# First gate unit of the two gated MLPs computed by token halves, in 128-column products

## The chip, the cores and the metric

The kernel runs on one core of one Trainium2 chip. The metric is device microseconds of one execution. The kernel before takes 1236.24 us, the median of 3 runs (1235.91 to 1247.31).

## The reference

Two transformer blocks act on 256 tokens of width 1024, batch 1, in float32. The second block is the one that the change touches:

```python
def swiglu(h, w_gate, w_up, w_down):
    return (jax.nn.silu(h @ w_gate) * (h @ w_up)) @ w_down
...
        h = modulate(rmsnorm(x, norm_ffn1[l]), sh1, sc1)
        x = x + 0.5 * g1[:, None, :] * swiglu(h, ffn1_w_gate[l], ffn1_w_up[l], ffn1_w_down[l])
        h = modulate(rmsnorm(x, norm_mix[l]), sh2, sc2)
        x = x + g2[:, None, :] * hybrid_mixer(h, ...)
        h = modulate(rmsnorm(x, norm_ffn2[l]), sh3, sc3)
        x = x + 0.5 * g3[:, None, :] * swiglu(h, ffn2_w_gate[l], ffn2_w_up[l], ffn2_w_down[l])
    return rmsnorm(x, norm_final)
```

`rmsnorm` divides each token's row by its root mean square and multiplies by a weight; `modulate` is `h * (1 + scale) + shift` with one scale and one shift per channel. The gated MLPs (ffn1, ffn2) have an inner width of 2816.

## The kernel before

**Data.** The 256 tokens are two halves t = 0, 1 of 128, which lie on the 128 partitions of `x` and `xn` (tokens by channels). A stage's input is transposed into `ah` and `al` (channels by tokens, 8 tiles of 128 channels): `ah` is the value rounded to fp32r, `al` the rest. Weights are cut into units of 128 x 2048 and split in the same way into `whi` and `wlo`: ScalarE (ACT) writes `whi` (L593), VectorE (DVE) then writes `wlo` (L1039). Each matrix product is three products, `whi*ah`, `whi*al` and `wlo*ah`, with a weight load of its own each. Three units are held at a time, units are split in program order, and the second unit of ffn1 is split on both engines only after the whole input of ffn1 is ready (`splits(U_FFN1 + 1)`).

**A unit of the gate or the up matrix** is `a_unit` (L1782 to L1784): two blocks of 128 output channels, each 8 channel tiles of 3 products with 256 columns (all tokens), so 48 products. The products go into one PSUM bank. The pairs of channel tiles wait for `in_ready`, one by one, in the first block.

**The entry of a gated MLP.** The part before ends with four quarters of the residual, (t, v) = (0,0), (0,1), (1,0), (1,1) with v a half of the channels. DVE adds each to `x` (ffn1: `gained_parts`, L1299, with the product by the final norm's weight, L1302; ffn2: `gated_part`, L1351, L1352). ACT squares each with a running sum (`part_squares`; in ffn1 two squares a quarter, L657 and L661, in ffn2 one). After the second quarter of a token half comes the root chain: small DVE operations (`part_rstd`, L1275 to L1285) with a square root on ACT (L668) in their midst. Then the token half is scaled: t = 0 by ACT (L703), t = 1 half by ACT and half by DVE (L1289). TensorE (PE) makes the gate's rows (L2050), then runs `part_T`: it transposes token half 0 three times over, 24 transposes (L1900) whose results are overwritten, and then both token halves, 16 transposes (L1881), into banks 4 to 7. After each pair of channel tiles ACT multiplies by the modulation's gain and adds the shift, 2 operations of 256 columns into `tmp2`, which holds two pairs (L638), and DVE casts to `ah` and subtracts for `al` (L1101, L1102), 512 columns each. PE's first product waits for the first pair.

**The mixer's entry** has another form already: the first pair of channel tiles of token half 0 goes ahead. `half_gained` (ACT, L678, 2 operations of 128 columns) stands between the two squares of token half 1, `half_split` (DVE, L1110, L1111, 256 columns each) after the last residual addition and ahead of the root chain, and PE starts products with it (L2208) before token half 1 is transposed (L2217).

Each engine takes its instructions strictly in the order in which they are written; semaphores join them.

Of the kernel before, what the change touches and what calls it, by code (L numbers as in the profile page):

```python
# [7 lines left out]
ALU = mybir.AluOpType  # L8
# [7 lines left out]
P = 128  # L16
# [73 lines left out]
Y_BANK = [[5, 6], [4, 7]]  # L90
PART = {"ffn1": 0, "mix": 1, "ffn2": 2, "out": 3}
# [17 lines left out]
def build(nc, t_in, out):  # L109
    g = t_in  # L110
    with ExitStack() as ctx:
# [472 lines left out]
        def _(act):  # L584
# [37 lines left out]
            def gained(stage_name, dst, gain, shift=None, npairs=4, bank_of=TBANK, ntiles=CT, first=0):  # L622

                for j in range(first, npairs):
# [4 lines left out]
                    for q in range(n):  # L629
                        c = 2 * j + q  # L630
                        n0 = P if stage_name == "mix" and j == 0 else 0
# [42 lines left out]
            def half_gained(gain, shift):  # L674

                act.wait_ge(half_tr, 1)
                for c in range(2):
                    ins = A.activation(tmp2[:, 0, c * S:c * S + P], ps[:, TBANK[0], c * S:c * S + P], ACT.Identity,  # L678
                                       scale=gain(c), bias=shift(c))
                ins.then_inc(half_hi, 1)  # L680

            def part_square(b, t, v):

                cols = slice(512 * v, 512 * v + 512)
                act.wait_ge(x_part, 4 * b + 2 * t + v + 1)
                return A.activation(xn[:, t, cols], x[:, t, cols], ACT.Square, scale=D ** -0.5,
                                    accum_out=sums[:, 2 * t + v:2 * t + v + 1])

            def part_norm(b, ahead=None):

                root_table()
                for t in range(TT):
                    if ahead and t == 1:
                        splits(U_TAIL + 1)
                        part_square(b, t, 0)
                        half_gained(*ahead)
                        part_square(b, t, 1).then_inc(sq_part, 1)
                    else:
                        part_squares(b, t)
                    root(b, t)  # L700
                    act.wait_ge(r_part, 2 * b + t + 1)
# [90 lines left out]
            def chunk(cs, used_units, b, silu, buf):  # L792
# [6 lines left out]
                if silu:  # L799
                    A.activation(hr, bank(b), ACT.Silu).then_inc(gated, 1)  # L800
# [98 lines left out]
            part_norm(PART["ffn1"])  # L899
            act.wait_ge(mod_done, 3)  # L900
            mod = lambda k: (lambda c: mgain[:, k, c:c + 1], lambda c: modT[:, k, c:c + 1])
            gained("ffn1", ah, *mod(0))
# [102 lines left out]
            part_norm(PART["ffn2"])  # L1005
# [16 lines left out]
        def _(dve):  # L1022
# [65 lines left out]
            def gained(stage_name, hi, lo, gain, shift=None, npairs=4, bank_of=TBANK, ntiles=CT, first=0):  # L1088

                for j in range(first, npairs):  # L1090
                    dve.wait_ge(in_hi, PAIR0[stage_name] + j + 1)
                    if stage_name == "mix" and j == 0:
                        ins = half_split(1)
# [12 lines left out]
            def half_split(t):  # L1106

                tt = slice(t * P, t * P + P)
                v = tmp2[:, 0].rearrange("p (c n) -> p c n", c=2)[:, :, tt]
                link(V.tensor_copy(ah[:, 0:2, tt], v))  # L1110
                return V.tensor_tensor(al[:, 0:2, tt], v, ah[:, 0:2, tt].bitcast(F32), ALU.subtract)  # L1111
# [180 lines left out]
            def gained_parts(idx, k):  # L1292

                dve.wait_ge(nb_landed, 16)
                for t in range(TT):
                    for v in range(2):
# [57 lines left out]
            def gated_parts(idx, b):  # L1354

                for t in range(TT):
                    gated_part(idx, b, t)
                    if t == 1 and b == PART["mix"]:
                        dve.wait_ge(half_hi, 1)
                        half_split(0).then_inc(half_in, 1)  # L1360
                    part_rstd(b, t)
                part_scale(b)

# [392 lines left out]
        def _(pe):  # L1756
# [350 lines left out]
            def swiglu(n0, c0, stage_name, gates):  # L2107
# [23 lines left out]
                pair(n0, None, c0, 4, stage_name)  # L2131
# [65 lines left out]
            part_T(PART["ffn1"])  # L2197
# [14 lines left out]
            def mix_T(t, cs, ready=None):  # L2212
                for c in cs:
                    if ready and c in ready:
                        pe.wait_ge(*ready[c])
# [185 lines left out]
```

## Time and profile before

| | us |
|---|---|
| median of 3 runs | 1236.24 |
| lowest, highest | 1235.91, 1247.31 |
| profiled execution | 1238.66 |
| its span, first to last instruction | 1237.0 |
| PE busy | 1201.1 |
| DVE busy | 828.4 |
| ACT busy | 597.9 |
| mean granted clock of PE | 0.993 |

The profile is of one execution. A product's length in it is the time from its start until its result has landed; products are pipelined, so what one costs in a run of products is the distance between two starts. PE is TensorE's products, PEld its weight loads. "Idle before, <- engine tile line" says how long the engine stood still and what ended the wait.

### The profile page before, as it was taken

Reading aid. Unit: us, or ns where it says so; the run is one execution under the profiler, and the core shown is the slowest. Engines: PE = TensorE matmul, PEld = TensorE weight load, DVE = VectorE, ACT = ScalarE, POOL = GpSimd, SP = SyncE. Lnnn points to the kernel's source line nnn. Section 1 sums busy time; section 2 is a strip of 40 time slices with the busy share of each in tenths; the row PEclk is TensorE's granted clock in tenths of the full one; section 3 lists DMA queues with packets and bytes.
Section 4 is the critical chain, followed back from the end, with each engine's and each line's share of the span. In section 5 each row is a group of like instructions: output and inputs, shape, how many; then the busy total and the mean of one; then the engine's idle time right before and its main releaser. Section 6 shows DMA issues by size and latency. Waiting matters only on the chain.

```text
span 1237.0 us, 19961 instructions
## 1 busy us (share of the span) xinstructions
PE 1201.1 (97%) x7963; PEld 1091.9 (88%) x7963; DVE 828.4 (67%) x1113; ACT 597.9 (48%) x789; POOL 70.4 (6%) x106
## 2 busy tenths in 40 slices
PE   8999999999999999999999999999998999999997
PEld 7897899999888889999979999998987888999996
DVE  6676777777766769777665654547985866554445
ACT  5545543444545554444365344446746745443433
POOL 9100011110000001111000000000000000000000
PEclk9999999999999999999999999999998999999999
DMA  7633699888363259888544555544561043565560
GB/s 247 220 132 109 211 334 306 302 288 280 113 205 125 81 204 337 287 290 301 178 137 170 188 188 183 176 155 161 187 205 69 1 170 115 195 201 172 175 213 35
DMA packets 143240, 236.38 MB, mean 191 GB/s; under 512 B 6357, under 2 KB 106950, under 8 KB 143174
## 3 DMA queue, kind: packets, MB, share of 16 engines
q1 hardware_dynamic: 130402, 196.73, 47.7%
q0 software_dynamic: 10400, 37.77, 8.6%
q10 hardware_dynamic: 2372, 0.96, 0.3%
q8 instruction: 46, 0.75, 0.3%
q14 instruction: 20, 0.16, 0.0%
HBM read 234.37 MB, written 1.05 MB: 190 GB/s over the span
## 4 chain that ended last, share of the span: by engine, by line
PE 90%; DVE 5%; ACT 3%; issue 1%; DMA 0%; DVEq 0%; ACTq 0%
PE ps L1782 13%; PE ps L1784 13%; PE ps L1783 13%; PE ps L1857 10%; PE ps L1859 10%; PE ps L1861 10%; PE ps L1794 2%; PE ps L1796 2%; PE ps L1795 2%; PE ps L1946 1%; PE ps L2043 1%; PE ps L1948 1%; PE ps L1947 1%; PE ps L2028 1%; PE ps L1821 1%
## 5 line engine op out<-in xcount | busy, mean ns | idle before, releaser
L1039 DVE TENSOR_TENSOR wlo<-raw,whi 128x2048 fp32r<-128x2048 f32 (+2 forms) x187 | 421.4, 2259 | 187.2 <-ACT whi L593 186.7
L593 ACT ACTIVATE whi<-raw 128x2048 fp32r<-128x2048 f32 (+2 forms) x187 | 352.6, 1888 | 246.5 <-PE ps L1861 146.5
L1782 PE MATMUL ps<-ah,whi 128*128 128x256 f32 x1392 | 396.1, 285 | 9.9 <-DVE al L1102 3.8
L1783 PE MATMUL ps<-al,whi 128*128 128x256 f32 x1392 | 394.5, 283 | 0.0
L1784 PE MATMUL ps<-ah,wlo 128*128 128x256 f32 x1392 | 394.5, 283 | 0.0
L1782 PEld LDWEIGHTS ps<-ah,whi 128*128 128x128 f32 x1392 | 267.6, 192 | 14.5 <-issue 6.9
L1783 PEld LDWEIGHTS ps<-al,whi 128*128 128x128 f32 x1392 | 267.6, 192 | 1.8
L1784 PEld LDWEIGHTS ps<-ah,wlo 128*128 128x128 f32 x1392 | 267.6, 192 | 0.0
L1857 PE MATMUL ps<-whi,hh 128*128 128x512 f32 x376 | 117.2, 393 | 0.0
L1859 PE MATMUL ps<-wlo,hh 128*128 128x512 f32 x376 | 116.3, 390 | 0.0
L1861 PE MATMUL ps<-whi,hl 128*128 128x512 f32 x376 | 115.9, 389 | 0.0
L1859 PEld LDWEIGHTS ps<-wlo,hh 128*128 128x128 f32 x376 | 70.6, 188 | 15.2
L1861 PEld LDWEIGHTS ps<-whi,hl 128*128 128x128 f32 x376 | 70.6, 188 | 15.2
L1428 DVE SCALAR_TENSOR_TENSOR stage<-stage,cact 128x1024 f32<-128x1024 f32 x63 | 80.7, 1281 | 1.4
L1857 PEld LDWEIGHTS ps<-whi,hh 128*128 128x128 f32 x376 | 67.5, 189 | 11.2
L804 ACT ACTIVATE work<-ps 128x512 f32<-128x512 f32 x32 | 19.2, 598 | 115.3 <-PE ps L1784 115.3
L566 POOL DMA_DIRECT2D stage<-in_w_ada_dram x72 | 38.3, 532 | 445.2 <-PE ps L1981 154.6
L800 ACT ACTIVATE work<-ps 128x512 f32<-128x512 f32 x22 | 13.2, 599 | 87.9 <-PE ps L1784 87.9
L1375 DVE TENSOR_TENSOR hl<-work,hh 128x512 fp32r<-128x512 f32 x54 | 37.4, 692 | 18.1 <-ACT hh L802 16.9
L1370 DVE TENSOR_TENSOR work<-work,ps 128x512 f32<-128x512 f32 x22 | 15.1, 687 | 50.9 <-ACT work L800 50.9
L716 ACT ACTIVATE work<-ps,nmx 128x128 f32<-128x128 f32 x40 | 14.7, 368 | 63.8 <-DVE nmx L1138 63.8
L1857 PE MATMUL ps<-whi,ah 128*128 128x512 f32 x120 | 37.3, 381 | 0.0
(392 smaller groups left out, 1666.3 us busy)
## 6 DMA issues: line engine op xcount, KB each, us to landing
stage<-in_w_ada_dram POOLq DMA_DIRECT2D x72, 512.0 KB, 6.6
raw<-in_w_up_dram SPq DMA_DIRECT2D x32, 1024.0 KB, 6.9
raw<-in_w_down_dram SPq DMA_DIRECT2D x32, 1024.0 KB, 7.6
raw<-in_ffn_w_gate_dram SPq DMA_DIRECT2D x22, 1024.0 KB, 5.1
raw<-in_ffn_w_up_dram SPq DMA_DIRECT2D x22, 1024.0 KB, 5.1
raw<-in_ffn_w_down_dram SPq DMA_DIRECT2D x22, 1024.0 KB, 5.0
raw<-in_moba_w_qkv_dram SPq DMA_DIRECT2D x11, 1024.0 KB, 7.0
raw<-in_w_in_dram SPq DMA_DIRECT2D x10, 1024.0 KB, 5.0
```

The source lines that it names most:

```text
L566: pool.dma_start(aslot[:, c % ADA_RING], ada[:, c, bass.ds(b * D, D)]).then_inc(a_landed[c % ADA_RING], 16)
L593: A.activation(whi[:, s, 0:size], raw[:, s, 0:size], ACT.Copy).then_inc(w_hi, 1)
L1039: V.tensor_tensor(wlo[:, s, 0:size], raw[:, s, 0:size], whi[:, s, 0:size].bitcast(F32), ALU.subtract).then_inc(w_lo, 1)
L1375: V.tensor_tensor(flat(hl[:, buf]), hs, flat(hh[:, buf]).bitcast(F32), ALU.subtract).then_inc(h_ready, 1)
L1428: V.scalar_tensor_tensor(aacc, v, cact[:, c:c + 1], aacc, ALU.mult, ALU.add).then_inc(a_sum, 1)
L1782: T.matmul(o, wmh, xh[:, c], start=(c == 0), stop=False)
L1783: T.matmul(o, wmh, xl[:, c], start=False, stop=False)
L1784: ins = T.matmul(o, wml, xh[:, c], start=False, stop=(c == CT - 1))
L1794: T.matmul(o, wmh, xh[:, c], start=(c == 0), stop=False)
L1857: T.matmul(o, xh[:, c, tt], wh[:, k, v:e], start=(first and k == 0), stop=False)
L1859: T.matmul(o, xh[:, c, tt], wl[:, k, v:e], start=False, stop=False)
L1861: ins = T.matmul(o, xl[:, c, tt], wh[:, k, v:e], start=False, stop=(last and k == kn - 1))
```

## The change

In ffn1 and ffn2 the first unit of the gate matrix is computed in four blocks of 128 output channels by 128 tokens (`ffn_entry`): block(channels 0, tokens 0), then the transposes of token half 1, then block(1, 0), block(0, 1), block(1, 1), each 24 products of 128 columns. Its result goes into bank 2 in place of bank 4. The 24 extra transposes go; token half 0 is transposed once. Token half 0 of all four pairs is scaled, shifted and split ahead: on ACT `half_gained` for pairs 0 and 1 between the squares of (1,0) and (1,1), pair 2 behind the squares of (1,1), pair 3 behind the root; on DVE pairs 0, 1 and 2 behind the last residual addition and ahead of the root chain, pair 3 behind the scaling. The scaling and splitting of token half 1 keeps its place and its number of operations, in 128 and 256 columns in place of 256 and 512. The mixer's entry does the same work as before.

```diff
+HALF_BASE = {0: 0, 1: 4, 2: 5}
+HALVES = {"ffn1": 4, "mix": 1, "ffn2": 4}
...
-            def half_gained(gain, shift):
-
-                act.wait_ge(half_tr, 1)
-                for c in range(2):
-                    ins = A.activation(tmp2[:, 0, c * S:c * S + P], ps[:, TBANK[0], c * S:c * S + P], ACT.Identity,
+            def half_gained(b, j, gain, shift):
+
+                act.wait_ge(half_tr, HALF_BASE[b] + j + 1)
+                if j >= 2:
+                    act.wait_ge(half_in, HALF_BASE[b] + j - 1)
+                for q in range(2):
+                    c = 2 * j + q
+                    ins = A.activation(tmp2[:, j % 2, q * S:q * S + P], ps[:, TBANK[j], q * S:q * S + P], ACT.Identity,
                                        scale=gain(c), bias=shift(c))
                 ins.then_inc(half_hi, 1)
...
-                    if ahead and t == 1:
-                        splits(U_TAIL + 1)
+                    if t == 1:
+                        if b == PART["mix"]:
+                            splits(U_TAIL + 1)
                         part_square(b, t, 0)
-                        half_gained(*ahead)
+                        half_gained(b, 0, *ahead)
+                        if b != PART["mix"]:
+                            half_gained(b, 1, *ahead)
                         part_square(b, t, 1).then_inc(sq_part, 1)
+                        if b != PART["mix"]:
+                            half_gained(b, 2, *ahead)
                     else:
                         part_squares(b, t)
                     root(b, t)
+                    if t == 1 and b != PART["mix"]:
+                        half_gained(b, 3, *ahead)
...
+            def half_ahead(b, j):
+
+                dve.wait_ge(half_hi, HALF_BASE[b] + j + 1)
+                half_split(j, 0).then_inc(half_in, 1)
...
+                    if t == 1:
+                        for j in range(3):
+                            half_ahead(0, j)
                     part_rstd(0, t)
                 part_scale(0)
+                half_ahead(0, 3)
...
-            def part_T(b):
+            def half_T(t, cs, ready=None):
+                for c in cs:
+                    if ready and c in ready:
+                        pe.wait_ge(*ready[c])
+                    o = ps[:, TBANK[c // 2], (c % 2) * S + t * P:(c % 2) * S + (t + 1) * P]
+                    ins = T.transpose(o, xn[:, t, c * P:(c + 1) * P], ident[:])
+                    if c % 2 == 1:
+                        ins.then_inc(tr_done if t else half_tr, 1)
+
+            def ffn_entry(b, n, stage_name):
+
+                wh, wl = w_view(whi, slot(n), CT, AW), w_view(wlo, slot(n), CT, AW)
+
+                def block(m, t):
+                    tt = slice(t * P, (t + 1) * P)
+                    o = ps[:, 2, m * S + t * P:m * S + (t + 1) * P]
+                    for c in range(CT):
+                        if m == 0 and c % 2 == 0:
+                            pe.wait_ge(in_ready if t else half_in, (PAIR0[stage_name] if t else HALF_BASE[b]) + c // 2 + 1)
+                        wmh, wml = wh[:, c, m * P:(m + 1) * P], wl[:, c, m * P:(m + 1) * P]
+                        T.matmul(o, wmh, ah[:, c, tt], start=(c == 0), stop=False)
+                        T.matmul(o, wmh, al[:, c, tt], start=False, stop=False)
+                        ins = T.matmul(o, wml, ah[:, c, tt], start=False, stop=(c == CT - 1))
+                    return ins
 
                 pe.wait_ge(xn_act, 2 * b + 1)
-                for _ in range(3):
-                    for c in range(CT):
-                        T.transpose(ps[:, TBANK[c // 2], (c % 2) * S:(c % 2) * S + P], xn[:, 0, c * P:(c + 1) * P],
-                                    ident[:])
-                transposes(xn, [(xn_act, 2 * b + 1), {0: (xn_dve, b + 1), 4: (xn_act, 2 * b + 2)}])
+                half_T(0, range(CT))
+                unit_wait(n)
+                pe.wait_ge(x_part, 4 * b + 3)
+                block(0, 0)
+                half_T(1, range(CT), {0: (xn_dve, b + 1), 4: (xn_act, 2 * b + 2)})
+                block(1, 0)
+                block(0, 1)
+                block(1, 1).then_inc(w_used, 1)
...
-                pair(n0, None, c0, 4, stage_name)
+                ffn_entry(PART[stage_name], n0, stage_name)
+                a_unit(n0 + 1, slot(n0 + 1), 5, ah, al)
```

The order of the instructions shows it on two engines. On ACT, at the entry of ffn1, from the scaling of token half 0 to the split of the second weight unit (`stage,sums` is the square's scratch and its sum, `newt` the small values of the root chain, `work` is `tmp2`), before:

```order
L703 ACTIVATE xn<-xn,newt 128x1024
L657 ACTIVATE stage,sums<-x 128x512
L661 ACTIVATE stage,sums<-xn 128x512
L657 ACTIVATE stage,sums<-x 128x512
L661 ACTIVATE stage,sums<-xn 128x512
L668 ACTIVATE newt<-newt 128x1
L703 ACTIVATE xn<-xn,newt 128x512
L638 ACTIVATE work<-ps,modT,mgain 128x256 x8
L593 ACTIVATE whi<-raw 128x2048
```

and now:

```order
L720 ACTIVATE xn<-xn,newt 128x1024
L691 ACTIVATE stage,sums<-x 128x512
L695 ACTIVATE stage,sums<-xn 128x512
L683 ACTIVATE work<-ps,modT,mgain 128x128 x4
L691 ACTIVATE stage,sums<-x 128x512
L695 ACTIVATE stage,sums<-xn 128x512
L683 ACTIVATE work<-ps,modT,mgain 128x128 x2
L670 ACTIVATE newt<-newt 128x1
L683 ACTIVATE work<-ps,modT,mgain 128x128 x2
L720 ACTIVATE xn<-xn,newt 128x512
L640 ACTIVATE work<-ps,modT,mgain 128x128 x8
L595 ACTIVATE whi<-raw 128x2048
```

Four of the new operations stand ahead of the last squares, two between them and the root.

On DVE, at the same place, from the last residual quarter to the scaling of token half 1, before:

```order
L1299 SCALAR_TENSOR_TENSOR x<-ps,rsq,x 128x512
L1302 TENSOR_TENSOR xn<-x,nB 128x512
L1275 TENSOR_SCALAR newt<-sums 128x1
L1276 TENSOR_SCALAR newt<-sums 128x1
L1277 TENSOR_SCALAR newt<-newt 128x1
```

and now:

```order
L1321 SCALAR_TENSOR_TENSOR x<-ps,rsq,x 128x512
L1324 TENSOR_TENSOR xn<-x,nB 128x512
L1127 CAST ah<-work 128x2x128
L1128 TENSOR_TENSOR al<-work,ah 128x2x128
L1127 CAST ah<-work 128x2x128
L1128 TENSOR_TENSOR al<-work,ah 128x2x128
L1127 CAST ah<-work 128x2x128
L1128 TENSOR_TENSOR al<-work,ah 128x2x128
L1297 TENSOR_SCALAR newt<-sums 128x1
L1298 TENSOR_SCALAR newt<-sums 128x1
L1299 TENSOR_SCALAR newt<-newt 128x1
```

The six operations of three half pairs stand between the residual and the root chain of token half 1.

## Rows read from the trace of the kernel before

**Rows 1.** The page, part 4: shares of the span in the chain that ended last

```profile
PE 90%; DVE 5%; ACT 3%; issue 1%; DMA 0%; DVEq 0%; ACTq 0%
```

**Rows 2.** Timeline, PE, first entry: start, length, engine, line, op, tiles, [idle before]

```profile
640.97 1.88 PE L2050 MATMUL ps<-stage,cum 128*128 128x512 f32 x4
...
642.68 2.78 PE L1900 MATMUL ps<-ident,xn 128*128 128x128 f32 x24
...
646.99 1.09 PE L1881 MATMUL ps<-ident,xn 128*128 128x128 f32 x8 [0.65 <-DVE xn L1289]
...
649.88 0.36 PE L1782 MATMUL ps<-ah,whi 128*128 128x256 f32 x1 [1.80 <-DVE al L1102]
...
657.48 0.28 PE L1782 MATMUL ps<-ah,whi 128*128 128x256 f32 x1
...
657.60 0.28 PE L1783 MATMUL ps<-al,whi 128*128 128x256 f32 x1
```

**Rows 3.** Timeline, PE, entry of the second gated MLP

```profile
1036.07 1.91 PE L1881 MATMUL ps<-ident,xn 128*128 128x128 f32 x16
...
1039.72 0.36 PE L1782 MATMUL ps<-ah,whi 128*128 128x256 f32 x1 [1.74 <-DVE al L1102]
...
1046.69 0.28 PE L1782 MATMUL ps<-ah,whi 128*128 128x256 f32 x1
```

**Rows 4.** Timeline, PE: pairs of 512 and 176 columns, then pairs of 512

```profile
851.26 0.51 PE L1859 MATMUL ps<-wlo,ah 128*128 128x512 f32 x2
...
851.60 0.51 PE L1861 MATMUL ps<-whi,al 128*128 128x512 f32 x2
...
990.50 0.61 PE L1857 MATMUL ps<-whi,bh 128*128 128x512 f32 x2
...
990.95 0.62 PE L1859 MATMUL ps<-wlo,bh 128*128 128x512 f32 x2
```

**Rows 5.** Timeline, weight loads: two products of 64 columns a row

```profile
970.73 0.30 PEld L2357 LDWEIGHTS ps<-stage,work 128*128 128x128 f32 x2
...
970.95 0.30 PEld L2358 LDWEIGHTS ps<-stage,work 128*128 128x128 f32 x2
```

**Rows 6.** Timeline, all engines, mixer entry: its half pieces, then the first product

```profile
840.86 0.79 ACT L678 ACTIVATE work<-ps,modT,mgain 128x128 f32<-128x128 f32 x2
...
841.54 0.62 ACT L686 ACTIVATE xn<-x 128x512 f32<-128x512 f32 x1
...
841.68 0.29 DVE L1110 CAST ah<-work 128x256 fp32r<-128x256 f32 x1 [0.46 <-ACT work L678]
...
842.00 0.42 DVE L1111 TENSOR_TENSOR al<-work,ah 128x256 fp32r<-128x256 f32 x1
...
842.35 0.21 DVE L1279 TENSOR_SCALAR newt<-sums 128x1 f32<-128x1 f32 x1
...
842.58 0.55 PE L2208 MATMUL ps<-whi,ah 128*128 128x512 f32 x2 [1.28 <-DVE al L1111]
```

**Rows 7.** Timeline, ACT, first entry: third of the four squares of the second token half

```profile
643.52 0.61 ACT L657 ACTIVATE stage<-x 128x512 f32<-128x512 f32 x1
```

**Rows 8.** Timeline, DVE, first entry: start of the second root chain, scale that follows

```profile
644.89 0.21 DVE L1275 TENSOR_SCALAR newt<-sums 128x1 f32<-128x1 f32 x1 [0.79 <-ACT stage L661]
...
646.45 0.49 DVE L1289 TENSOR_SCALAR xn<-xn,newt 128x512 f32<-128x512 f32 x1
```

**Rows 9.** Windows, first entry: stretch, its us, each engine's busy time, PEclk, DMA share, GB/s

```profile
650.00:655.00 5.00, 4.98 (x28) 4.77 (x29) 4.16 (x7) 4.96 (x7) 0.00 (x0) 0.66 0.00 0
```

**Rows 10.** Timeline, second entry: last square (ACT), root chain and scale (DVE)

```profile
1033.38 0.63 ACT L657 ACTIVATE xn<-x 128x512 f32<-128x512 f32 x1 [1.24 <-DVE x L1352]
...
1034.14 0.21 DVE L1279 TENSOR_SCALAR newt<-sums 128x1 f32<-128x1 f32 x1 [0.79 <-ACT xn L657]
...
1035.32 0.49 DVE L1289 TENSOR_SCALAR xn<-x,newt 128x512 f32<-128x512 f32 x1
```

**Rows 11.** Timeline, DVE, first entry: low parts of the second and third weight units

```profile
653.75 2.29 DVE L1039 TENSOR_TENSOR wlo<-raw,whi 128x2048 fp32r<-128x2048 f32 x1 [0.65 <-ACT whi L593]
```

More of the change, by code:

```diff
@@ L630, in gained @@
                         c = 2 * j + q
-                        n0 = P if stage_name == "mix" and j == 0 else 0
+                        n0 = P if j < HALVES.get(stage_name, 0) else 0
                         src = ps[:, bank_of[j], q * S + n0:(q + 1) * S]
@@ L685, in part_square @@
                 act.wait_ge(x_part, 4 * b + 2 * t + v + 1)
-                return A.activation(xn[:, t, cols], x[:, t, cols], ACT.Square, scale=D ** -0.5,
-                                    accum_out=sums[:, 2 * t + v:2 * t + v + 1])
+                ins = A.activation(fscr[:, 2 * t + v] if b == 0 else xn[:, t, cols], x[:, t, cols], ACT.Square,
+                                   scale=D ** -0.5, accum_out=sums[:, 2 * t + v:2 * t + v + 1])
+                if b == 0:
+                    act.wait_ge(xg_part, 2 * t + v + 1)
+                    ins = A.activation(fscr[:, 4 + 2 * t + v], xn[:, t, cols], ACT.Square, scale=D ** -0.5,
+                                       accum_out=sums[:, 4 + 2 * t + v:5 + 2 * t + v])
+                return ins
             def part_norm(b, ahead=None):
@@ L799, in chunk @@
                 if silu:
-                    A.activation(hr, bank(b), ACT.Silu).then_inc(gated, 1)
+                    A.activation(hr, bank(2 if isinstance(cs, int) and cs in (CHUNK0["ffn1"], CHUNK0["ffn2"]) else b), ACT.Silu).then_inc(gated, 1)
                     act.wait_ge(h_sq, cs1)
@@ L898, in _ @@
             splits(U_FFN1)
-            part_norm(PART["ffn1"])
             act.wait_ge(mod_done, 3)
             mod = lambda k: (lambda c: mgain[:, k, c:c + 1], lambda c: modT[:, k, c:c + 1])
+            part_norm(PART["ffn1"], mod(0))
             gained("ffn1", ah, *mod(0))
@@ L1004, in _ @@
             splits(U_FFN2)
-            part_norm(PART["ffn2"])
+            part_norm(PART["ffn2"], mod(2))
             gained("ffn2", ah, *mod(2))
@@ L1091, in gained @@
                     dve.wait_ge(in_hi, PAIR0[stage_name] + j + 1)
-                    if stage_name == "mix" and j == 0:
-                        ins = half_split(1)
+                    if j < HALVES.get(stage_name, 0):
+                        ins = half_split(j, 1)
                     elif shift is None:
@@ L1357, in gated_parts @@
                     gated_part(idx, b, t)
-                    if t == 1 and b == PART["mix"]:
-                        dve.wait_ge(half_hi, 1)
-                        half_split(0).then_inc(half_in, 1)
+                    if t == 1:
+                        for j in range(1 if b == PART["mix"] else 3):
+                            half_ahead(b, j)
                     part_rstd(b, t)
                 part_scale(b)
+                if b == PART["ffn2"]:
+                    half_ahead(b, 3)
             def chunk(cs, b, silu, buf):
@@ L2196, in _ @@
             gate_rows(0, (0, 1))
-            part_T(PART["ffn1"])
             swiglu(U_FFN1, CHUNK0["ffn1"], "ffn1", 1)
@@ L2210, in tail_half, with warm_T @@
                 return ins
[L2212 removed]
+            def warm_T(cs):
                 for c in cs:
[L2214 to L2220 removed]
+                    o = ps[:, TBANK[c // 2], (c % 2) * S:(c % 2) * S + P]
+                    T.transpose(o, xn[:, 0, c * P:(c + 1) * P], ident[:])
             mix = PART["mix"]
             pe.wait_ge(xn_act, 2 * mix + 1)
[L2224 removed]
+            half_T(0, range(2))
             for _ in range(2):
[L2226 removed]
+                warm_T(range(2, CT))
             unit_wait(U_TAIL)
[L2228 removed]
+            pe.wait_ge(half_in, HALF_BASE[mix] + 1)
             tail_half(0)
[L2230 removed]
+            half_T(1, range(CT), {0: (xn_dve, mix + 1), 4: (xn_act, 2 * mix + 2)})
             pe.wait_ge(in_ready, PAIR0["mix"] + 1)
@@ L2371, in _ @@
             gate_rows(2, (0, 1))
-            part_T(PART["ffn2"])
             swiglu(U_FFN2, CHUNK0["ffn2"], "ffn2", 3)
```

20 lines of the change are left out of this document (6 added, 14 removed).

## The prediction

> **What bounds the kernel now.** I read five views. First the shares of the chain of waits: 90% of the span's chain is TensorE (PE), 5% DVE, 3% ACT [rows 1]. So time is won only where PE stands still or does empty work, and every us of added PE work counts. Second, the timeline of PE at the two entries. In ffn1 it makes 24 empty transposes, waits 0.65 us for token half 1, transposes it, and waits 1.80 us until the first product at 649.88; the 48 products of the first gate unit end where the second unit starts, at 657.48 [rows 2]. In ffn2 the 16 transposes start at 1036.07, PE waits 1.74 us, the first product starts at 1039.72, the second unit at 1046.69 [rows 3]. These two starts, 657.48 and 1046.69, are my measuring points: behind them the instructions are the same, so what they move by, the end moves by. Third, the timelines of ACT and DVE, for the chain that leads there. Fourth, rows of short products, for the price of 128 columns. Fifth, a window with the granted clock.
>
> **Price of a 128-column product.** At full clock, products of 256 columns start 0.12 us apart [rows 2]. A pair of 512 columns takes 0.45 us, 0.227 each, and a pair of 512 and 176 takes 0.34, which leaves 0.113 for 176 columns [rows 4]. Products of 64 columns start 0.22 / 2 = 0.11 apart [rows 5]. 24 transposes of 128 columns take 2.78 us and 16 take 1.91, so (2.78 - 1.91) / 8 = 0.109 from start to start, and 0.27 for one from start to end [rows 2, 3]. Below 256 columns the price hardly falls: each product has a weight load of 128 columns, and that seems to be the floor. So 0.112 for 128 columns. The lower bound is the slope of 512 to 256 columns, (0.227 - 0.12) / 256 per column, which gives 0.12 - 0.053 = 0.067; I take the floor, since the 64- and 176-column rows lie on either side of 128. The upper bound is two passes: the two float32 products of the gate's rows are recorded as four [rows 2], so 2 x 0.112 = 0.224; 176 columns show nothing of it. The unit then costs 96 x 0.112 = 10.8 us in place of 48 x 0.12 = 5.8: 5.0 us more PE work per entry, of which only what runs in former idle time is free.
>
> The Trainium skill (TensorE: Matmul & The Clock Gate, Back-to-back issue gap) gives about 81 ns for a product of 128 columns in a stream of loads and products. By that figure, as an estimate, the 78 products behind the last wait would take 2.4 us less at each entry, and the first rival's limit would set the sum, +2.3 us. The same page (LDWEIGHTS) puts a load at its columns divided by 1.2, 107 ns for 128; the trace agrees with this one, 0.11 us at 64 columns.
>
> **What the half pieces cost on ACT and DVE.** The mixer's entry shows them: the two ACT operations of a pair take 0.68 us until the next starts (840.86 to 841.54), 0.79 with their end; DVE's two take 0.67 until the next (841.68 to 842.35) and 0.74 with their end; PE starts 0.16 later [rows 6].
>
> **First entry (ffn1).** PE's transposes of half 0 start at 642.68 as before; a pair is there 0.11 + 0.27 later, 643.06. ACT: pair 0 takes the place of the third square at 643.52 [rows 7], pair 1 goes at 644.20, the two squares at 644.88 and 645.49 (0.61 each), pair 2 at 646.10, with its end at 646.89. DVE waits for that piece with the root chain queued behind it: cast at 646.91, root chain at 647.59 in place of 644.89 [rows 8], **2.70 us later**, so the scaling of half 1 starts at 646.45 + 2.70 = 649.15. ACT's pair 3 lies between root and scaling and is done by 649.2. DVE's pair 3 is queued behind the scaling, whose pitch I estimate at 0.42 from its 0.49: 649.57, end 650.31, PE at 650.47. PE meanwhile did pair 0 at 645.24, pair 1 at 645.92, pair 2 at 647.82, and stood still between: it starts 4.6 us earlier than before, but cannot pass 650.47. Behind it: 6 products 0.67, 8 transposes 0.87, 72 products 8.06, and the unit ends at 650.47 + 9.60 = 660.07. Against 657.48: **+2.6 us**. The pieces of half 1 are no bound: the first pair is transposed at 651.5, ACT and DVE end the fourth at about 655.3, PE needs it at 656.7.
>
> In these 2.6 the half clock of the kernel before is counted as gone: in 650 to 655 the mean granted clock was 0.66 [rows 9], that is 3.4 of the 5 us at the lower level (1.2 GHz in place of 2.4), behind the waits of 0.65 and 1.80 us [rows 2]; they cost up to 1.7 us.
>
> **Second entry (ffn2).** Half 0 is transposed from 1036.07 - 24 x 0.109 = 1033.45 on, its first pair is there at 1033.83. ACT: pairs 0 and 1 go at 1033.90 and 1034.58, since the last square's data is there only at 1033.38 but stands behind them: the square starts at 1035.26 in place of 1033.38 [rows 10]. Pair 2 follows at 1035.87, ends at 1036.66; DVE's root chain starts at 1036.68 + 0.67 = 1037.35 in place of 1034.14 [rows 10], **3.21 us later**, the scaling at 1038.53, pair 3's end at 1038.95 + 0.74, PE at 1039.85. Plus 9.60: 1049.45 against 1046.69, **+2.8 us**. Here the 24 empty transposes held the real ones back (half 1 was scaled from 1035.32 on, its transposes started at 1036.07 + 8 x 0.109 = 1036.94), and that gain of 1 us is in the sum.
>
> **What else moves.** Second weight unit: its split on ACT stands behind the input, now at about 654.5, `wlo` at 656.4 to 658.7 (656.04 before [rows 11]); PE comes at 660.1, so it is covered by 1.4 us, as before by 657.48 - 656.04. That cover is gone if the products are cheap (first rival). DMA: the loads behind wait for these splits and move with them, 2.7 us later, as PE does. SP and POOL issue nothing new. ACT's eight operations more per entry (4 pairs x 0.68) are paid back by eight narrower ones later; all of it is in the chain above. The waits for `mod_done`, bank 2 and the gate's copy: done before 643, cost nothing. Mixer's entry: nothing.
>
> **Sum:** 2.6 + 2.8 = +5.4 us. Against the profiled execution 1238.66 -> 1244.1; against the median 1236.24 -> **1241.6**. The profiled execution lies 2.4 us above the median, and I predict the median.
>
> **The rivals.**
> 1. *Cheap products* (0.067 to 0.08): 78 products behind the last wait, up to 3.5 us saved an entry, PE would end the unit at 656.6 to 657.6. But `wlo` of the second unit is then late: the input's last pieces end about 0.3 us earlier and it is ready at 658.5, in ffn2 at 1048.0: +1.0 and +1.3, so +2.3 us, 1238.5. The 81 ns of the Trainium skill's page (TensorE: Matmul & The Clock Gate, Back-to-back issue gap) lead to the same place. Against it speaks [rows 5]. 11%.
> 2. *Not slower: the half pieces slip in.* If ACT and DVE found room for them and the root chain of half 1 kept its old time, pair 3 would let PE go at 646.45 + 0.42 + 0.74 + 0.16 = 647.8 and at 1036.6; plus 9.60, the ends are 657.4 and 1046.2, -0.1 and -0.5: 1235.6. It decides where the root chain is delayed by less than 0.1 us and not by 2.7. Against it: ACT is gapless from one square to the next in ffn1, and DVE's queue is strict. 7%.
> 3. *The clock.* PE now has holes (646.6 to 647.8, 648.5 to 650.5, the like in ffn2) and could be granted half clock behind them, as it was behind the holes of the kernel before [rows 9]. A 3.4 us stretch costs up to 1.7 if loads slow down too, nothing if the floor stays; one at each entry, up to +3.4 on the sum: 1245.0. 20%.
> 4. *Two passes* for products below a width: 78 x 0.112 = 8.7 more at each entry, 5.4 + 17.5 = +22.9: 1259.1. Against it: 176 columns at 0.113. 5%.
>
> The forecast has 57%. A measurement of this kernel can tell about 1% (12 us) from no change. Only rival 4 leaves this band.
>
> **The numbers.** Predicted 1241.6. The range 1237.0 to 1247.0 takes in the forecast, rivals 1 and 3 and 2 us of a run's scatter; rivals 2 and 4, 12%, and a little scatter are outside. Faster by over 1%: 1%; within 1%: 93%; slower by over 1%: 6%.
>
> **What would show it.** In the new trace: starts of 128-column products 0.11 apart (0.067: rival 1; 0.22: rival 4); the first at about 645.2; the scaling of half 1 at 649.15 and 1038.5 (646.5 and 1035.3: rival 2); PE waiting for DVE's fourth half pair until 650.5; the second unit at 660.1 and 1049.4, with no wait for `wlo` (with one: rival 1); a granted clock of 1.0 in 650 to 660 and 1040 to 1050 (rival 3 otherwise). The forecast is wrong if the second unit starts before 658.5 at the first entry, or if a wait behind it swallows the delay.

## The result and the profile after

The changed kernel takes **1259.03 us** (median of 4 runs, 1253.86 to 1261.58), the kernel before 1236.08 in the same session (4 runs, 1234.17 to 1247.31). The ratio on record for the runs is 1.0149, interval 1.0101 to 1.0197 (that of the two medians is 1.0186): slower. The prediction was 1241.6, so it missed by 17 us. The profiled execution is the fastest of the four, 1253.86 us, granted clock 0.986; the others have 0.982 and 0.980 (twice).

From the page of the changed kernel: busy time, the granted clock in 40 slices, the chain of waits.

```profile
span 1252.2 us, 20092 instructions
PE 1213.3 (97%) x8011; PEld 1104.9 (88%) x8011; DVE 831.2 (66%) x1129; ACT 601.4 (48%) x805; POOL 69.6 (6%) x106
...
PEclk9999999999999999999987999999999999999999
...
PE 90%; DVE 5%; ACT 3%; issue 1%; DMA 0%; DVEq 0%; ACTq 0%
```

The chain is as before [rows 1]: no new wait took over. But PE is busy 12.2 us longer (1201.1 before), and two slices of the clock fall to 8 and 7. They cover 626 to 689 us, and ffn1 begins there.

The traces have to be laid over each other first. DVE's first residual addition of the entry, before and after:

```profile
636.03 0.74 DVE L1299 SCALAR_TENSOR_TENSOR x<-ps,rsq,x 128x512 f32<-128x512 f32 x1
```

```profile
635.13 0.74 DVE L1321 SCALAR_TENSOR_TENSOR x<-ps,rsq,x 128x512 f32<-128x512 f32 x1
```

So a forecast for the first entry has 0.90 taken off before it is held against this trace. PE there (start, length, engine, line, operation, [idle before]):

```profile
644.34 0.30 PE L1943 MATMUL ps<-ah,whi 128*128 128x128 f32 x1 [1.52 <-DVE al L1128]
644.48 0.28 PE L1944 MATMUL ps<-al,whi 128*128 128x128 f32 x1
644.59 0.28 PE L1945 MATMUL ps<-ah,wlo 128*128 128x128 f32 x1
...
646.87 0.33 PE L1943 MATMUL ps<-ah,whi 128*128 128x128 f32 x1 [0.99 <-DVE al L1128]
...
649.48 0.47 PE L1943 MATMUL ps<-ah,whi 128*128 128x128 f32 x1 [1.73 <-DVE al L1128]
649.75 0.42 PE L1944 MATMUL ps<-al,whi 128*128 128x128 f32 x1
649.97 0.42 PE L1945 MATMUL ps<-ah,wlo 128*128 128x128 f32 x1
...
650.82 1.93 PE L1928 MATMUL ps<-ident,xn 128*128 128x128 f32 x8
...
667.80 0.52 PE L1810 MATMUL ps<-ah,whi 128*128 128x256 f32 x1
```

The first products start 0.11 apart, as forecast. Behind the third hole they start 0.21 to 0.22 apart, and at that pace PE goes through all the rest of the unit. The windows (stretch, its us, busy times, PEclk, DMA share, GB/s) say why; before, only one of them was low, at 0.66 [rows 9]:

```profile
645.00:650.00 5.00, 2.28 (x17) 2.00 (x16) 3.04 (x12) 2.65 (x8) 0.00 (x0) 0.80 0.01 3
650.00:655.00 5.00, 5.00 (x25) 5.00 (x25) 2.31 (x7) 3.31 (x9) 0.00 (x0) 0.50 0.00 0
...
665.00:670.00 5.00, 5.00 (x25) 5.00 (x25) 0.00 (x0) 0.00 (x0) 0.00 (x0) 0.50 0.23 77
670.00:675.00 5.00, 5.00 (x37) 5.00 (x36) 0.00 (x0) 0.00 (x0) 0.00 (x0) 0.81 0.01 3
```

PE is granted 1.2 GHz for 23.9 us on end (twice the missing share of each window: 2.0, four times 5, 1.9). The fall comes at 648.0, inside the third hole (PE stands still from 647.75 to 649.48), and from 649.48 on PE is busy all the time. DVE at this entry, the second root chain, the scaling behind it, and the low part of the second weight unit:

```profile
646.73 0.21 DVE L1297 TENSOR_SCALAR newt<-sums 128x1 f32<-128x1 f32 x1
...
648.28 0.48 DVE L1311 TENSOR_SCALAR xn<-xn,newt 128x512 f32<-128x512 f32 x1
```

```profile
656.54 2.29 DVE L1056 TENSOR_TENSOR wlo<-raw,whi 128x2048 fp32r<-128x2048 f32 x1 [1.04 <-ACT whi L595]
```

The second entry stands 10.80 us later than before (gate's rows, L2104, at 1042.54; before, L2050, at 1031.74):

```profile
1046.42 0.30 PE L1943 MATMUL ps<-ah,whi 128*128 128x128 f32 x1 [1.12 <-DVE al L1128]
...
1050.58 0.36 PE L1943 MATMUL ps<-ah,whi 128*128 128x128 f32 x1 [1.36 <-DVE al L1128]
1050.74 0.41 PE L1944 MATMUL ps<-al,whi 128*128 128x128 f32 x1
...
1054.07 0.32 PE L1943 MATMUL ps<-ah,whi 128*128 128x128 f32 x1
1054.22 0.27 PE L1944 MATMUL ps<-al,whi 128*128 128x128 f32 x1
```

```profile
1061.82 0.34 PE L1810 MATMUL ps<-ah,whi 128*128 128x256 f32 x1
```

```profile
1048.19 0.21 DVE L1301 TENSOR_SCALAR newt<-sums 128x1 f32<-128x1 f32 x1
...
1049.37 0.49 DVE L1311 TENSOR_SCALAR xn<-x,newt 128x512 f32<-128x512 f32 x1
```

Here the low stretch lasted only 3.4 us (window 1050 to 1055: 0.66), and the clock rose again while 128-column products ran.

**Where the 15.2 us between the two spans went.** First entry: the second unit starts at 667.80 + 0.90 against 657.48 [rows 2], +11.2; its first products still run at half clock until 671.75, 0.213 apart for 0.12, +1.7. Second entry: 1061.82 - 10.80 against 1046.69 [rows 3], +4.3. That is 17.2. Back come 0.9 that this execution was ahead from the start, and about 1 us because a low stretch of 6.8 us at 944 to 951 in the trace of before was only 3.4 us long here.

### The profile page after: what moved, and what is told of

The parts are those of the page before. It is cut to its first block, busy times and chain, and to the rows that moved or that the text cites. A ratio compares the mean times of both kernels' runs of the same rounds, so it can differ in the third digit from the quotient of the medians.

```text
span 1252.2 us, 20092 instructions
## 1 busy us (share of the span) xinstructions
PE 1213.3 (97%) x8011; PEld 1104.9 (88%) x8011; DVE 831.2 (66%) x1129; ACT 601.4 (48%) x805; POOL 69.6 (6%) x106
## 4 chain that ended last, share of the span: by engine, by line
PE 90%; DVE 5%; ACT 3%; issue 1%; DMA 0%; DVEq 0%; ACTq 0%
PE ps L1810 13%; PE ps L1812 13%; PE ps L1811 13%; PE ps L1885 10%; PE ps L1887 10%; PE ps L1889 10%; PE ps L1822 2%; PE ps L1824 2%; PE ps L1823 2%; PE ps L2000 1%; PE ps L2097 1%; PE ps L2002 1%; PE ps L2001 1%; PE ps L2082 1%; PE ps L1849 1%
## 5 line engine op out<-in xcount | busy, mean ns | idle before, releaser
L1810 PE MATMUL ps<-ah,whi 128*128 128x256 f32 x1360 | 386.7, 284 | 6.7 <-DVE al L1115 2.6
L1812 PE MATMUL ps<-ah,wlo 128*128 128x256 f32 x1360 | 385.6, 284 | 0.0
L1811 PE MATMUL ps<-al,whi 128*128 128x256 f32 x1360 | 385.6, 284 | 0.0
L1810 PEld LDWEIGHTS ps<-ah,whi 128*128 128x128 f32 x1360 | 261.6, 192 | 10.0 <-issue 3.0
L1811 PEld LDWEIGHTS ps<-al,whi 128*128 128x128 f32 x1360 | 261.6, 192 | 1.8
L1812 PEld LDWEIGHTS ps<-ah,wlo 128*128 128x128 f32 x1360 | 261.5, 192 | 0.0
L1889 PEld LDWEIGHTS ps<-whi,hl 128*128 128x128 f32 x376 | 70.6, 188 | 15.2
L1885 PEld LDWEIGHTS ps<-whi,hh 128*128 128x128 f32 x376 | 67.5, 189 | 11.2
```

Source lines behind the costliest of these rows:

```text
L1810: T.matmul(o, wmh, xh[:, c], start=(c == 0), stop=False)
L1811: T.matmul(o, wmh, xl[:, c], start=False, stop=False)
L1812: ins = T.matmul(o, wml, xh[:, c], start=False, stop=(c == CT - 1))
L1885: T.matmul(o, xh[:, c, tt], wh[:, k, v:e], start=(first and k == 0), stop=False)
L1889: ins = T.matmul(o, xl[:, c, tt], wh[:, k, v:e], start=False, stop=(last and k == kn - 1))
```

## The experiments

Theory: the clock. The half pieces cut holes into PE's work, the granted clock falls there, and a stream of 128-column products doesn't bring it back soon. Rivals: the extra columns or the delay by the half pieces are larger than the sum had them. All ratios are to the kernel before on the same chip. "Fillers" are products of 512 columns into a bank that nobody reads by then.

**The change, its holes filled.**

```diff
+FILL = {0: 5, 4: 4, 6: 7}
...
+                def fill(k):
+                    for _ in range(k):
+                        T.matmul(ps[:, 3], whi[:, slot(n), 0:P], whi[:, slot(n), 0:512], start=True, stop=True)
...
+                        if m == 0 and t == 0 and c in FILL:
+                            fill(FILL[c])
```

PE also waits for the last residual addition before the unit (`x_part` 4 in place of 3), since that addition reads the bank that the fillers overwrite; the other variants with fillers do the same.

> The change with its 96 products a unit, and PE's holes ahead of pairs 0, 2 and 3 filled with 5, 4 and 7 products of 512 columns into a bank whose content is overwritten later (0.227 us each by the rows of before). Theory (clock): the change lost its time to a half clock that begins behind these holes and does not end while 128-column products run. Filled, the granted clock stays 1.0 in both entries, 128-column products start 0.11 us apart, the second unit starts 2.6 to 3.3 us later than before at each entry: 1241 to 1243 us. Rival (short products or the half pieces cost it by themselves, whatever the clock): the time stays at 1253 to 1260 us.

Measured: 1242.07 us (10 runs), ratio 1.0052 (1.0017 to 1.0086). Timeline of PE and a window at the first entry:

```profile
642.91 1.39 PE L1939 MATMUL ps<-whi 128*128 128x512 f32 x5
644.54 0.33 PE L1950 MATMUL ps<-ah,whi 128*128 128x128 f32 x1 [0.23 <-DVE al L1129]
...
647.87 1.84 PE L1939 MATMUL ps<-whi 128*128 128x512 f32 x7
649.76 0.33 PE L1950 MATMUL ps<-ah,whi 128*128 128x128 f32 x1
649.93 0.28 PE L1951 MATMUL ps<-al,whi 128*128 128x128 f32 x1
```

```profile
650.00:655.00 5.00, 5.00 (x47) 5.00 (x47) 2.76 (x8) 3.88 (x9) 0.00 (x0) 1.00 0.00 0
```

The second weight unit at both entries:

```profile
659.37 0.33 PE L1811 MATMUL ps<-ah,whi 128*128 128x256 f32 x1
...
1050.32 0.33 PE L1811 MATMUL ps<-ah,whi 128*128 128x256 f32 x1
```

The same 128-column products after the same stages of ACT and DVE, 0.11 apart and at full clock. More work on PE made the changed kernel 17.0 us faster. What is left, 6 us, is about what the sum had priced. Counted from the gate's rows (640.36 and 1032.36 here, 640.97 and 1031.74 before), the second unit starts 2.5 us later than before at the first entry and 3.0 at the second; the sum had 2.6 and 2.8.

**Only the half pieces, only the narrow products.** First the change with its unit in 48 products of 256 columns behind all transposes:

```diff
-                block(0, 0)
                 half_T(1, range(CT), {0: (xn_dve, b + 1), 4: (xn_act, 2 * b + 2)})
-                block(1, 0)
-                block(0, 1)
-                block(1, 1).then_inc(w_used, 1)
+                pe.wait_ge(half_in, HALF_BASE[b] + 4)
+                whole(0)
+                whole(1).then_inc(w_used, 1)
```

> The change's work on ACT and DVE kept as it is, but PE computes the first gate unit in 48 products of 256 columns, once all pieces of both halves are there. Theory (clock): PE stands still for longer than in the change, the clock may fall, but with 256 columns it is back after about 3.4 us as in the kernel before; the unit ends 0.4 to 2.2 us later than before at each entry: 1237 to 1241 us. Rival (the holes alone make the long half clock): the low clock lasts some 20 us here too, 1246 to 1258 us.

Then the kernel before with nothing but its first unit in 96 products of 128 columns:

```diff
-                pair(n0, None, c0, 4, stage_name)
+                narrow_unit(n0, slot(n0), 4, ah, al, stage_name)
+                a_unit(n0 + 1, slot(n0 + 1), 5, ah, al)
```

> The kernel before with one thing of the change alone: the first gate unit in 96 products of 128 columns, in four blocks, started when it started before; ACT, DVE, the empty transposes and every wait as before. Theory (clock): at full clock 96 x 0.111 in place of 48 x 0.12 is +4.9 less what is hidden behind the first waits, about +3.5 an entry; where the clock falls at the entry (first entry in the profile of before) it stays low until products of 256 columns run, for 20 us or more, another +8 to +11: 1243 us with no such stretch, 1251 to 1254 with one, 1262 with two. Rival (the delay of the half pieces on ACT and DVE costs the time): about 1243 us and a low clock for 3.4 us at most.

Measured: only the half pieces 1242.48 us (10 runs), ratio 1.0057 (1.0023 to 1.0091); only the narrow products 1264.53 us (4 runs), ratio 1.0210 (1.0147 to 1.0272). Windows of the first, then of the second:

```profile
645.00:650.00 5.00, 0.99 (x5) 1.03 (x6) 3.04 (x12) 3.04 (x9) 0.00 (x0) 0.52 0.00 0
650.00:655.00 5.00, 4.50 (x22) 4.13 (x21) 3.04 (x9) 4.82 (x10) 0.00 (x0) 0.50 0.01 3
655.00:660.00 5.00, 5.00 (x42) 5.00 (x42) 4.31 (x2) 3.70 (x3) 0.00 (x0) 0.96 0.29 93
...
975.00:980.00 5.00, 4.83 (x26) 4.69 (x25) 2.25 (x6) 2.44 (x7) 0.00 (x0) 0.63 0.00 2
980.00:985.00 5.00, 5.00 (x25) 5.00 (x23) 2.45 (x5) 2.19 (x6) 0.00 (x0) 0.50 0.00 0
```

```profile
650.00:655.00 5.00, 4.65 (x25) 4.39 (x26) 4.28 (x5) 5.00 (x5) 0.00 (x0) 0.66 0.00 0
655.00:660.00 5.00, 5.00 (x26) 5.00 (x25) 2.37 (x2) 1.74 (x2) 0.00 (x0) 0.50 0.70 243
...
1055.00:1060.00 5.00, 5.00 (x25) 5.00 (x25) 4.47 (x2) 4.08 (x4) 0.00 (x0) 0.50 0.26 66
```

With 256 columns even the longest hole (6.07 us, until 649.00) goes with a low clock of 10.2 us at the first entry, 3.8 of them inside the hole, and 6.8 at the second. With 128 columns and the waits of the kernel before it lasts 20.5 us at both (from 651.6 and from 1054.4 on). So the half pieces aren't needed for the loss; the narrow products behind the waits that the kernel before has are enough. The median of the first, 1242.48, misses its expected 1237 to 1241: six of its ten runs lie at 1239.1 to 1243.2, four at 1250.4 to 1250.5, and the profile is of one of those four. Its windows hold what the expectation hadn't: a third stretch of 20.5 us, from 976.3 on, in the state-space stage of the mixer, which none of these edits touches.

**PE alone.** 200 products of 128 columns once behind a pause and once behind 120 products of 256 columns:

```python
run(60, 512, 0)   # then a pause of about 10 us
run(200, 128, 1); run(60, 256, 2)   # then a pause
run(120, 256, 3); run(200, 128, 4)
```

> Nothing of the model is computed; PE alone runs, each product with a weight load: 60 products of 512 columns; pause of about 10 us; 200 of 128 columns, then 60 of 256; pause; 120 of 256, then 200 of 128; pause; 60 of 512, then 60 of 128. Theory (clock): behind the first pause the 200 products of 128 columns start 0.213 us apart at half clock to their end (43 us), and the clock rises only in the 60 of 256; behind the second pause the clock rises within some 4 us of the 256 columns, and the 200 of 128 behind them start 0.111 apart at full clock (22 us) and keep it. Rival: 128-column products regain the clock as the wider ones do, within about 4 us, so that most of the first 200 start 0.111 apart.

Measured: 173.39 us (one run). The first narrow product behind the pause, and windows:

```profile
33.23 3.04 PE L151 MATMUL ps<-xr,wr 128*128 128x128 f32 x13 [10.14 <-DVE scr L137]
```

```profile
75.00:80.00 5.00, 5.00 (x25) 5.00 (x25) 0.00 (x0) 0.00 (x0) 0.50 0.00 0
80.00:85.00 5.00, 5.00 (x42) 5.00 (x42) 0.00 (x0) 0.00 (x0) 0.95 0.00 0
...
100.00:110.00 10.00, 10.00 (x82) 10.00 (x82) 0.00 (x0) 0.00 (x0) 0.95 0.00 0
110.00:125.00 15.00, 15.00 (x135) 15.00 (x135) 0.00 (x0) 0.00 (x0) 1.00 0.00 1
```

The clock fell in the pause (at 25.8). From 33.23 on the narrow products run without a gap, 0.213 apart, for 42.7 us, and never get the clock back; the 256-column products behind them have it from about 80.5 on. Behind the second pause 256 columns come first and the clock is back about 5.5 us after they begin (95.48). The same 200 narrow products then keep it: 135 in 15 us, 0.111 each. So in this one run 200 narrow products neither raised a low clock nor lowered a high one. That they can see a rise, the second entry of the change shows (1054.07).

**Fillers under each half.** The same two kernels as above, with fillers: `fill(n, 27 if b == 0 else 20)` and `fill(n, 5)` ahead of the 256-column products, `fill(n, 8)` ahead of the narrow ones.

> The half pieces on ACT and DVE as in the change, 48 products of 256 columns on PE, and the holes at both entries filled with 512-column products (27 and 20 ahead of the transposes of token half 1, 5 behind them), so that no low clock should begin there. It prices the half pieces alone. Theory (the prediction's sum, at full clock): half 1 is scaled 2.7 and 3.2 us later, its pieces are narrower, the second unit starts 0.4 and 0.5 us later than before, in all 1236 to 1238 us with the granted clock at 1.0 in both entries. Rival (what the change loses at full clock is the chain of half pieces, not the columns): +2.6 and +2.8 us, 1241 us.

> The kernel before with the first gate unit in 96 products of 128 columns, as in the experiment before, and 8 products of 512 columns in the hole ahead of the first. It prices the columns alone at full clock. Theory (clock): no low clock at the entries; 96 x 0.111 = 10.7 from 649.88 on, the second unit starts about 3.1 and 3.7 us later than before, 1241 to 1243 us, against 1264.5 without the 16 fillers. Rival (the narrow products themselves bring the clock down, holes or not): 1255 us and more.

Measured: half pieces with fillers 1237.70 us (10 runs), ratio 1.0004 (0.9976 to 1.0032). At the measuring points, counted from the gate's rows, its second unit starts 0.5 and 0.7 us later than before, as expected (0.4 and 0.5). Narrow products with fillers 1254.46 us (4 runs: 1245.43, 1254.41, 1254.51, 1275.24), ratio 1.0111 (1.0054 to 1.0169; the last run isn't in it). PE of the narrow one:

```profile
647.34 2.09 PE L1913 MATMUL ps<-whi 128*128 128x512 f32 x8
...
651.60 0.33 PE L1798 MATMUL ps<-ah,whi 128*128 128x128 f32 x1 [0.36 <-DVE al L1102]
...
652.66 0.47 PE L1798 MATMUL ps<-ah,whi 128*128 128x128 f32 x1 [0.18 <-DVE al L1102]
```

The second one misses the theory: 1241 to 1243 us was expected, and its median lies at the rival's 1255. Fillers ahead of the unit were not enough: inside it PE waits for each pair of channel tiles (0.36 and 0.18 us and shorter), and at 652.6 the clock falls all the same. That these waits are the reason is argued, not shown; for it speaks that the change with its holes filled and the gapless narrow row of PE alone kept the clock. Only the run at 1245.43 can be free of a long stretch, and its mean clock of 0.996 still leaves about 5 us more at the low level than the best runs of the kernel before have (0.998), so the price of the narrow products without any fall isn't read from it. The two at 1254.4 to 1254.5 lie about one stretch of 20 us at half clock (10 us) above it; the one at 1275.24, which is the profiled one, has three in its trace: 20.5 us at 652.6, 23.8 at 987.1 (in the state-space stage), 20.5 at 1065.6.

**Other forms of the entry.** The kernel before with both channel blocks of each pair of tiles done as it arrives, in 256 columns (banks 2 and 3); then the same with token half 0 transposed once and fillers in place of the empty transposes (24 of them; the expectation says 16):

```diff
+                for j in range(CT // 2):
+                    pe.wait_ge(in_ready, PAIR0[stage_name] + j + 1)
+                    for m in range(AW // P):
+                        o = ps[:, 2 + m, 0:S]
+                        for c in (2 * j, 2 * j + 1):
```

```diff
-                for _ in range(3):
-                    for c in range(CT):
-                        T.transpose(...)
+                f0, f1 = {0: (14, 8), 2: (6, 8)}[b]
...
+                fill(n, f0)
...
+                fill(n, f1)
```

In both, ACT's first `Silu` of a gated MLP reads the two banks.

> A version that may beat both: the kernel before, its first gate unit in 256-column products, but with both blocks of output channels computed for a pair of channel tiles as soon as the pair is there (12 products a pair in place of 6), into banks 2 and 3. The waits between pairs, 0.2 to 0.5 us each, go, and so does part of what lets the clock fall. The next bound is the low part of the second unit's weights, ready at 656.04 and about 1045.9. Expected: second unit 0.4 to 1.4 us earlier in ffn1, 0.7 in ffn2: 1233.5 to 1235 us beside a kernel before at 1235.7. Rival (the entry is bound by the weights' low part or by the clock anyway): no difference within 0.2%.

> The same, and token half 0 transposed once, with 512-column products in the holes in place of the 16 empty transposes (14 and 6 ahead of the transposes of half 1, 8 behind them). Theory (clock): no low clock in either entry, transposes of half 1 no longer held back in ffn2 (1.1 us): second unit 1.4 us earlier in ffn1 and 1.5 to 1.9 in ffn2, 1232 to 1234 us, and less scatter. Rival: empty transposes kept the clock as well as the fillers do, and the entries are bound by the weights: as the version without fillers.

Measured: 1235.72 us, ratio 1.0006 (0.9970 to 1.0042), and 1234.27 us, ratio 0.9990 (0.9963 to 1.0016), 12 runs each. PE no longer waits between the pairs, but then, in both, for the second weight unit. From the first:

```profile
652.55 2.29 DVE L1041 TENSOR_TENSOR wlo<-raw,whi 128x2048 fp32r<-128x2048 f32 x1 [0.65 <-ACT whi L593]
...
654.90 0.38 PE L1784 MATMUL ps<-ah,whi 128*128 128x256 f32 x1 [0.23 <-DVE wlo L1041]
```

Neither can be told from the kernel before, and both lie above what was expected (1233.5 to 1235, 1232 to 1234): the rivals' bound, the second unit's weights, is the one that the traces show. The second has 10 of 12 runs within 1233.8 to 1235.2 and two at 1242.7; the first has four of 12 at 1245.1 to 1246.6. The profile of the first has the waits of 0.65 and 1.80 us as the kernel before does, and yet a granted clock of 1.00 in 645 to 655.

**The scattered runs.** 16 of 74 runs of the kernel before lay at 1243 to 1247 us with a clock of 0.984 to 0.989 (a single run of 3264.72 us is not counted). Could that be the stretch in the state-space stage? Each pass over a head there has one product of 384 columns, one of 256 and six of 64. One more product of 384 columns in each pass over a head (16 passes in all; the expectation says 14, which leaves out the two ahead of the loop):

```diff
+                T.matmul(o, selr[:, h:h + 1].to_broadcast([P, P]), rowc[:], start=True, stop=True)
                 T.matmul(o, selr[:, h:h + 1].to_broadcast([P, P]), rowc[:], start=True, stop=False)
```

> The kernel before, with one more 384-column product ahead of the decay rows of each of the 14 passes over heads of the state-space stage; it writes a bank that the next product of the program overwrites. Theory: the long stretches at the lower granted clock, about 20 us long and begun at 976.8 us in the profile of the wide variant and at 987.7 us in that of the narrow variant with fillers, lie in that stage's 64-column products, and they are what puts 6 of 29 runs of the kernel before at 1243 to 1247 us. With the wide product in each pass they are gone: no run above 1240 us, and a median 0 to 2 us above the kernel before (14 products of at most 0.17 us). Rival: they have another cause. Then as many runs as before, about one in five, lie at 1243 us or above, and the rest stand 0 to 2 us higher.

> The variant whose first unit of both MLPs runs in 256-column products with its first token half transposed once and fillers ahead, with the same added 384-column product in each pass of the state-space stage. Theory: 1234 to 1236 us with no run above 1240 us (1233.8 to 1235.2 us in ten of twelve runs without it, and two at 1242.7 us that the added products take away). Rival: a run in six still lies at 1242 us or above, and the rest stand 0 to 2 us higher.

Measured: 1238.91 us (12 runs, 1235.85 to 1239.68), ratio 0.9992 (0.9966 to 1.0018), and **1236.19 us** (12 runs, 1235.15 to 1236.57), ratio **0.9970 (0.9944 to 0.9995)**. In the same session 7 of 23 runs of the kernel before were at 1243 or above (median 1237.49); of these 24 none was above 1239.7. At the rate of 16 in 74 that would happen by chance about 3 times in 1,000. The theory holds as far as times can say; in a profile of the kernel before itself the stretch was never caught. So the cause of the scattered runs is likely, not shown. The added products cost 1.3 us (1235.2 against 1233.9, each the best runs of its kernel at a clock of 0.997, in two sessions). The last kernel is the only one of all these that beats the kernel before, by 0.3%, and by its even runs, not by its best ones. But the 23 runs of the kernel before beside it hold more scattered ones (7 of 23) than its other runs do (9 of 51); against the medians of those, 1235.66 to 1236.10, 1236.19 is no gain.

## Why the prediction was wrong

**Price of a product, 0.112: right.** 0.111 measured, at the entry (644.48, 644.59) and in 135 products on end. The 81 ns of the Trainium skill's page (TensorE: Matmul & The Clock Gate, Back-to-back issue gap) didn't show in any run. Rival 1 is out.

**The half pieces: right to 0.1 us.** Root chain of half 1: forecast 647.59 - 0.90 = 646.69, measured 646.73; scaling 648.25, 648.28; first product 644.34, 644.34; fourth half pair passed 649.57, 649.48. At the second entry, with 10.80 added: root chain 1048.15, 1048.19; scaling 1049.33, 1049.37; fourth pair 1050.65, 1050.58. Rival 2 is out.

**Cover of the second weight unit: right at full clock.** With the holes filled `wlo` was done at 658.25 (655.96 + 2.29) and PE came at 659.37: covered by 1.1 us (forecast 1.4). In the change itself it was done at 658.8, 1.0 later than forecast in this trace's time (657.8), because the transposes of half 1 ran at half clock too (1.93 us for 8, in place of 1.06); PE came only at 667.8.

**Sum at full clock, +5.4: right.** With the holes filled the second unit starts 2.5 and 3.0 us later, +5.5 in all. By times, the changed kernel with fillers has 1240.1 to 1240.3 in its runs at a clock of 0.998 and 0.999, the kernel before 1234.1 to 1234.3 at 0.998: +6.0. The half pieces with 256 columns and fillers are +1.1 of it at the two measuring points and +2.1 by times (1236.3 at 0.998); the 128-column products are the rest, about 4 us.

**The clock: this step failed.** The working counted the half clock of the kernel before as gone, asked for 1.0 in 650 to 660, and gave rival 3 20% with the words "A 3.4 us stretch costs up to 1.7 if loads slow down too, nothing if the floor stays; one at each entry". Three things in it were wrong. (a) Two of the three holes were named (measured 1.52, 0.99 and 1.73 us), and [rows 9] had shown the clock fall behind holes of 0.65 and 1.80, while none followed the 1.74 of the second entry in that trace ([rows 3]; granted clock 1.00 from 1035 to 1050): one entry of two, so 20% was low. In the one profile of the change it fell at both. (b) Of the two cases for the floor, "nothing if the floor stays" is out: it went from 0.111 to 0.213, nearly double. (c) The length, and with it the price, was the term that was mis-sized: 3.4 us was copied from a place where 256-column products follow. In the change 78 narrow products and 8 transposes follow: from 649.48 to 667.80 PE took 18.3 us for what was priced at 9.60. That is 8.7 of the 11.2 us at this entry. A stretch of 20.5 to 23.9 us costs 10 to 12 us, and there can be one at each entry: the two runs at 1261.6 have 0.980 against the profiled run's 0.986, by 0.006 x 1260 x 2 about 15 us more at the low level, and are 7.7 us slower. No profile shows where these 15 us lie; the second entry is the likely place. The fillers gave back 17.0 us of the 23 between the medians.

The kernel before's trace could not have shown (c) in full: no row of 128-column products alone ran at half clock in it. But it held a longer stretch than the one copied, 6.8 us from 944.4 on, where products of 128 and 256 columns are mixed:

```profile
945.00:950.00 5.00, 5.00 (x22) 4.72 (x22) 1.59 (x4) 2.87 (x11) 0.00 (x0) 0.50 0.27 111
```

And it gave the bound. Had the low level been taken as possible for the whole unit, 78 more times 0.112 at each entry, rival 3's end would have been +17.5 on the sum, near 1259, and the range would have had to go there.

The measured 1259.03 is by chance the 1259.1 of rival 4 (two passes for each narrow product). That mechanism is refuted: at full clock narrow products start 0.11 apart. The number is near because half clock, where it lasts, doubles the price of the same products; in the profiled run it lasted through the unit at one entry only.

What the Trainium skill says of the clock (TensorE: Matmul & The Clock Gate, What's actually happening), "the default state is throttled, and activity releases the throttle", agrees with the rows of 256 columns that follow a low clock here (back 4.1 us behind their start in the change, 4.6 and 5.5 us in PE alone), and not with the 200 narrow products in a gapless row, 42.7 us without a rise.

**Still open:** what decides whether the clock falls, and for how long. Behind waits of 0.65 and 1.80 us, or 1.74 us, it fell at one entry of two in the profile of the kernel before and at none in that of the paired version. In one profile the clock rose after 3.4 us amid the narrow products (second entry of the change), in others after 20.5 or 23.9, and in PE alone not within 42.7 us. The number of changed kernel runs is small (4), so how often both entries are hit is not known.

## What to carry to other kernels

Be wary of a long row of narrow products behind a wait of the tensor engine: priced at full clock the unit and its half pieces cost 5 to 6 us, and at the clock that they really got 23. For every wait of the tensor engine, look at what runs behind it, and if it is a row of narrow products, price the whole row at the low level as well. If the waits can't go, fill them with wide empty products; here that was worth 17 us for 32 of them.

## What was not expected of the hardware

- A gapless stream of 128-column products, each with its weight load, stayed at 1.2 GHz for 42.7 us (one run); at 2.4 GHz the same stream stayed there for 22 us.
- At half clock products of 128 and of 256 columns start the same 0.213 us apart; at full clock 0.111 and 0.12.
- The state-space stage, mostly products of 64 columns, had 20.5 us at half clock in one profile (from 976.3), 23.8 in another (from 987.1) and none in the others, with the same instructions. With one more product of 384 columns in each head's pass none of 24 runs was above 1239.7, against 16 of 74 at 1243 to 1247 without.
- A fall came at 652.6 behind no longer waits than 0.36 and 0.18 us between groups of six narrow products, although eight 512-column products had run ahead of them.
